# Gate products with adjacent moving columns, eleven row groups inside the first gates, and all modulation in mixer 1

## What is computed

```python
s = jnp.einsum('thpd,hpnd->thpn', q, sub_keys)          # two lists of 128 key scores a head
s_top, i_top = lax.top_k(s, PEER_TOPK)                  # 16 of each
best, pos = lax.top_k(cand, PEER_TOPK)                  # 16 pairs
expert = jnp.take_along_axis(cand_idx, pos, axis=-1)
g = jax.nn.softmax(best, axis=-1)
act = jax.nn.gelu(jnp.einsum('td,thkd->thk', xb, u[expert]), approximate=False)
return jnp.einsum('thk,thkd->td', g * act, v[expert])
```

## Time and profile before

| | |
|---|---|
| median of 3 runs | 3645.04 us (3644.92 to 3646.84) |
| profiled execution, its span | 3653.25 us, 3651.1 us |
| PE, DVE, POOL, ACT busy | 93%, 66%, 37%, 36% |
| DMA moved | 908.08 MB, mean 249 GB/s |
| mixer 1, heads 0 to 7 | about 252 to 490 us |
| queries and choice, first gates, block loop of layer 1 | 600 to 758, to 864, to 1870 us |
| first gates, block loop of layer 2 | 2525 to 2631, to 3642 us |

### The profile page before, as it was taken

The page is one execution under the profiler, slowest core; times in us unless marked ns, Lnnn a source line. Parts: engine busy times, 40 slices in busy tenths (PEclk is TensorE's granted clock), DMA queues, the critical chain, the costliest instruction groups (busy, mean ns, idle before and its releaser), DMA issues. The chain is left out here.

```text
span 3651.1 us, 44818 instructions
## 1 busy us (share of the span) xinstructions
PE 3378.0 (93%) x16120; PEld 2179.6 (60%) x16120; DVE 2419.8 (66%) x5203; ACT 1317.9 (36%) x3289; POOL 1343.6 (37%) x1028
## 2 busy tenths in 40 slices
PE   6986889989999999998979998996999999999988
PEld 3434644367777777765534465454867777777654
DVE  1038643876887987887771233269578798888778
ACT  2122111145655555541010134113555555555200
POOL 0000000003666667776620000000156566687665
PEclk9998689989999999999989998997799999999999
DMA  3211213225999999999961110211399999999998
GB/s 116 92 46 69 70 64 144 99 93 191 383 375 362 386 397 397 409 409 409 409 268 69 52 64 12 104 47 53 99 353 390 347 403 382 394 409 409 409 409 356
DMA packets 271692, 908.08 MB, mean 249 GB/s; under 512 B 30536, under 2 KB 31192, under 8 KB 270960
## 3 DMA queue, kind: packets, MB, share of 16 engines
q0 software_dynamic: 147456, 536.94, 37.7%
q1 hardware_dynamic: 124016, 368.29, 26.7%
HBM read 900.90 MB, written 4.22 MB: 248 GB/s over the span
## 5 line engine op out<-in xcount | busy, mean ns | idle before, releaser
L671 PE MATMUL psum<-hT,mod 128*128 128x256 f32 x4096 | 985.3, 396 | 55.3 <-ACT big L1088 29.5
L671 PEld LDWEIGHTS psum<-hT,mod 128*128 128x128 f32 x4096 | 796.4, 199 | 185.0 <-issue 77.9
L1098 ACT ACTIVATE levels<-key_numbers,hT 128x128 bf16<-128x128 f32 x1712 | 543.3, 389 | 452.5 <-PE psum L707 342.7
L1847 POOL DMA_INDIRECT w<-in_peer_u,tmp x172 | 243.1, 1414 | 978.8 <-DVEq L1543 791.1
L1676 DVE SCALAR_TENSOR_TENSOR tmp<-w,small,tmp 128x1024 f32<-128x1024 f32 x339 | 435.6, 1285 | 67.5 <-DMA w<-in_peer_v,tmp 27.6
L707 PEld LDWEIGHTS psum<-x,levels 128*128 128x128 bf16 x6144 | 384.2, 116 | 148.1 <-issue 120.2
L1656 DVE CUSTOM_DVE_ANT_0 w<-w,hn 128x1024 f32<-128x1024 f32 x342 | 407.6, 1224 | 57.8 <-DMA w<-in_peer_u,tmp 28.3
L707 PE MATMUL psum<-x,levels 128*128 128x32 bf16 x6144 | 405.8, 238 | 34.5 <-issue 14.1
L1847 POOL DMA_INDIRECT big<-in_peer_down,tmp x86 | 120.5, 1401 | 833.3 <-DVEq L1543 703.0
L681 PE MATMUL psum<-rows,big 128*128 128x512 f32 x800 | 358.8, 592 | 0.7 <-DVE big L1612 0.7
L1101 ACT ACTIVATE levels<-levels 128x512 bf16<-128x512 bf16 x428 | 269.6, 630 | 13.6
(11 more groups left out here) (303 smaller groups left out, 4082.3 us busy)
## 6 DMA issues: line engine op xcount, KB each, us to landing
mod<-in_uT SPq DMA_DIRECT2D x256, 512.0 KB
rows<-in_peer_v SPq DMA_DIRECT2D x64, 512.0 KB
rows<-in_peer_up SPq DMA_DIRECT2D x64, 512.0 KB
w<-in_w_in SPq DMA_DIRECT2D x14, 2048.0 KB, 7.9
w<-in_ada_w SPq DMA_DIRECT2D x12, 2048.0 KB, 8.0
srow<-in_peer_v SPq DMA_DIRECT2D x32, 512.0 KB
tmp<-in_peer_v SPq DMA_DIRECT2D x32, 512.0 KB
srow<-in_peer_up SPq DMA_DIRECT2D x32, 512.0 KB
```

What stands on the lines that cost most here:

```text
L671: last = nc.tensor.matmul(ps[4 + e % 2][:, 0:ND], ub[e % UV][:, k, :], hT[:, k, ND:SEQ], start=k == 0, stop=k == KC - 1)
L1098: last = nc.scalar.activation(hits[n % HITS][:, j * P:(j + 1) * P], keyno, ACT.Abs, bias=nibT[:, n * BATCH + j:n * BATCH + j + 1])
L1847: nc.gpsimd.indirect_dma_start(ring[n % ROWS], None, table, bass.IndirectOffsetOnAxis(idx[:, c:c + 1], 0))\
```

## The change

It does five things. (1) `hot` is laid out (part, token, key), so that the 32 moving columns of a token lie side by side. (2) For that, `first_keys` holds the first key's number and the gate along the innermost dimension, and the table `key_rows` with its one cast falls away. (3) Eleven of the 128 units run inside the first gates, one every fourth batch from batch 20 (`first_units`); `unit_table` spreads the other 117 over the loop, with its costs as they were. (4) All twelve sections of modulation stand in mixer 1: two behind each of heads 0 to 3, one behind heads 4 to 7. (5) Layer 1 then does as layer 2 did: eight first products instead of four before the gates.

```diff
+FIRST_UNITS = 11
-def blocks_before(layer, n):
-    first = 4 if layer == 0 else 8
-    return first + (AHEAD - first) * n // BATCHES
+def blocks_before(n):
+    return 8 + (AHEAD - 8) * n // BATCHES
+def first_units(n):
+    return max(0, min(FIRST_UNITS, (n - 16) // 4))
...
-    share = (4 * GROUPS * 5.15 + sum(v[1] for v in room)) / sum(v[0] for v in room)
+    share = ((4 * GROUPS - FIRST_UNITS) * 5.15 + sum(v[1] for v in room)) / sum(v[0] for v in room)
...
-    return [round(4 * GROUPS * v / done) for v in table]
+    return [FIRST_UNITS + round((4 * GROUPS - FIRST_UNITS) * v / done) for v in table]
+def after_head(h):
+    return (2 * h, 2 * h + 1) if h < 4 else (h + 4,)
...
-        hot = [part(x_, 8 + 3 * b, 3, BF16).rearrange("p (r a t) -> p r a t", r=3, a=QA) for b in range(2)]
+        hot = [part(x_, 8 + 3 * b, 3, BF16).rearrange("p (r t a) -> p r t a", r=3, a=QA) for b in range(2)]
...
-                                                hot[n // 4 % 2][:, r, :, t], start=r == 0, stop=r == 2)
+                                                hot[n // 4 % 2][:, r, t, :], start=r == 0, stop=r == 2)
...
# PE, mixer 1
-                modulation(h)
+                for n in after_head(h):
+                    modulation(n)
...
# PE, behind layer 1's queries
-            modulation(8)
-            modulation(9)
-            modulation(10)
-            turn_picks(0, 0)
-            modulation(11)
-            turn_picks(0, 1)
-            for e in range(4):
-                first_product(0, e)
+            first_experts(0)
...
# ACT, mixer 1
-                    if l == 6 and h:
-                        modulation(h - 1)
+                    if l == 5 and h:
+                        modulation(after_head(h - 1)[0])
...
                     if h >= 1:
                         head_out(h - 1, P, 0, h, wide_sq, h - 1)
+                        if h <= 4:
+                            modulation(after_head(h - 1)[1])
...
# DVE, first_keys
-                    spreads(tt(hot_one, key_rows, first_no[q][:, c].unsqueeze(1).to_broadcast([P, QA, WIDE]), ALU.is_equal))
-                    tt(hot[m % 2], hot_one.unsqueeze(1).to_broadcast([P, 3, QA, WIDE]),
-                       g_part[:, :, c].unsqueeze(2).to_broadcast([P, 3, QA, WIDE]), ALU.mult).then_inc(ga_ready, 1)
+                    spreads(tt(hot_one, keyno16[:, 0:QA].unsqueeze(1).to_broadcast([P, WIDE, QA]),
+                               spread(first_no[q][:, c], [P, WIDE, QA]), ALU.is_equal))
+                    tt(hot[m % 2], hot_one.unsqueeze(1).to_broadcast([P, 3, WIDE, QA]),
+                       spread(g_part[:, :, c], [P, 3, WIDE, QA]), ALU.mult).then_inc(ga_ready, 1)
...
# DVE, loop over the 64 batches of the first gates
                     for _ in range(first_pieces(n - 1), first_pieces(n)):
                         next(chooser[0])
+                    for u in range(first_units(n - 1), first_units(n)):
+                        run_unit(layer, u)
```

More of the change, by code:

```diff
@@ L403, in build @@
         ada = cols(a["ada_w_2"], 12)
-        ada_at = [len(order) + n + (6 if n >= NH else 0) for n in range(12)]
-        order += ada[:NH] + cols(a["w_out"], 2) + cols(a["peer_w_q"], 4) + ada[NH:]
+        ada_at = [len(order) + n for n in range(12)]
+        order += ada + cols(a["w_out"], 2) + cols(a["peer_w_q"], 4)
         order += cols(a["w_in_2"], 7) + cols(a["w_out_2"], 2) + cols(a["peer_w_query_2"], 4)
-        OUT_FIRST = (15, 32)
+        OUT_FIRST = (19, 32)
         outputs = [0 if n in ada_at else 4 for n in range(len(order))]
@@ L506, in _ @@
                 second_block(0, e)
-            for n in range(19, 23):
+            for n in range(23, 25):
                 load_section(n)
-            for n in range(NH, 12):
-                modulation(n)
             expert_blocks(0)
@@ L791, in modulation @@
                 seen.next(ada_row_in, 16)
-                nc.tensor.matmul(ps[1][0:1, :], ones[0:1, 0:1], ada_b[n // NH], start=False, stop=True).then_inc(ada_done, 1)
+                nc.tensor.matmul(ps[1][0:1, :], ones[0:1, 0:1], ada_b, start=False, stop=True).then_inc(ada_done, 1)
             full, heads = slice(0, P), [slice(0, 64), slice(64, P)]
@@ L899, in _ @@
             queries(1)
-            pe.wait_ge(sc_used, 32)
-            for e in range(6):
-                first_product(1, e)
-            turn_picks(1, 0)
-            turn_picks(1, 1)
-            first_product(1, 6)
-            first_product(1, 7)
+            first_experts(1)
             dense_experts(1)
@@ L1114, in group_gelu, with first_acts, unit_gelu @@
                 nc.scalar.activation(g8[g % 2], a8[g % 2], ACT.Gelu).then_inc(act_out, 1)
+            def first_acts(layer):
+                block_gelu(layer, 0)
+                block_gelu(layer, 1)
+                gate_exp(DENSE[0])
+                block_gelu(layer, 2)
+                gate_exp(DENSE[1])
+                block_gelu(layer, 3)
+                for n in range(len(DENSE)):
+                    copy_picks(layer, n)
+                for e in range(4, 8):
+                    block_gelu(layer, e)
+            def unit_gelu(layer, u):
+                kind, g = unit(u)
+                if kind == "u":
+                    group_gelu(layer, g)
             def dense_acts(layer):
@@ L1123, in dense_acts @@
                     if n >= 5:
-                        for e in range(blocks_before(layer, n - 5), blocks_before(layer, n - 4)):
+                        for e in range(blocks_before(n - 5), blocks_before(n - 4)):
                             block_gelu(layer, e)
@@ L1127, in dense_acts @@
                         gate_exp(0)
+                    for u in range(first_units(n - 6), first_units(n - 5)):
+                        unit_gelu(layer, u)
                 copy_gates(layer, 0, WIDES - 1)
-                for e in range(blocks_before(layer, BATCHES - 5), AHEAD):
+                for e in range(blocks_before(BATCHES - 5), AHEAD):
                     block_gelu(layer, e)
+                for u in range(first_units(BATCHES - 6), FIRST_UNITS):
+                    unit_gelu(layer, u)
                 for e in range(NKEY):
                     for u in range(units_due(e - 2), units_due(e - 1)):
-                        kind, g = unit(u)
-                        if kind == "u":
-                            group_gelu(layer, g)
+                        unit_gelu(layer, u)
                     if e and e + AHEAD - 1 < NKEY:
@@ L1153, in _ @@
             queries(0)
-            modulation(8)
-            modulation(9)
-            gate_exp(DENSE[0])
-            modulation(10)
-            gate_exp(DENSE[1])
-            copy_picks(0, 0)
-            modulation(11)
-            copy_picks(0, 1)
-            for e in range(4):
-                block_gelu(0, e)
+            first_acts(0)
             dense_acts(0)
@@ L1571, in peer @@
                 dve.wait_ge(x_stored, 32 * (layer + 1))
-                spreads(nc.vector.tensor_copy(key_rows, spread(keyno[:, 0:QA], [P, QA, WIDE])))
                 dve.wait_ge(picks_copied, len(DENSE) * (layer + 1))
@@ L1631, in peer @@
                     for n in range(units_due(e - 1), units_due(e)):
-                        kind, g = unit(n)
-                        if kind == "u":
-                            score_rows(layer, g)
-                        else:
-                            add_rows(layer, g)
-                            if g % GROUPS == GROUPS - 1:
-                                finish_tile(layer, g // GROUPS, y)
+                        run_unit(layer, n)
                 dve.wait_ge(blk_summed, (layer + 1) * NKEY)
@@ L1647, in peer, with run_unit @@
                         step(stt(x[:, t, :], x[:, t, :], rs[:, t:t + 1], rows[:, 2, :], ALU.mult, ALU.mult), 0 if t == NT - 1 else t)
+            def run_unit(layer, n):
+                kind, g = unit(n)
+                if kind == "u":
+                    score_rows(layer, g)
+                else:
+                    add_rows(layer, g)
+                    if g % GROUPS == GROUPS - 1:
+                        finish_tile(layer, g // GROUPS, y)
             def score_rows(layer, g):
```

52 lines of the change are left out of this document (24 added, 28 removed).

## The result

| | before | changed |
|---|---|---|
| median of 4 runs | 3644.98 us (3643.91 to 3646.84) | 3591.97 us (3590.15 to 3592.26) |
| ratio | | 0.9853, 95% interval 0.9836 to 0.987 |
| profiled execution, its span | 3653.25, 3651.1 us | 3592.14, 3590.3 us |

The change is faster by 53 us where 24 were predicted. Of the page of the changed kernel two lines, against the earlier trace rows: the GB/s, and the gathers' queue.

The account below looks back on a forecast made before the run. It took PE to bound each block loop up to step 92, DMA close behind, then DMA. Mixer -2, first gates +37 and +43, loops -51 each gave -24: 3621 us from the median, range 3592 to 3686.

Parts of the forecast that it names:

- Moving columns adjacent: Gate products in the loop: a pair of weight load and product falls from 60 to 40 ns, 0.48 us a batch.
- rival 1: Gate products stay at 60 ns a pair because the weight load sets it: +39, 3684 us, slower; chance 0.22.
- Gate held along the innermost dimension: On DVE, a first_keys goes from 1.45 to about 2.5 us, +1.07, 16 times in first gates, 48 in the loop.
- Eleven units in the first gates: First gates become DVE-bound and longer: +37 us in layer 1, +43 in layer 2.
- The loop without them: Block loop with the eleven units moved out: early stage gains 39 us, late stage 12, together -51 in each layer.
- Modulation: Mixer 1 with the moved sections: +10 us against PE's gains at heads 1 to 4, sum about -2.
- rival 3: The held gate costs DVE nothing for hot: 34 us less than forecast, 3587 us; chance 0.06.
- Rival 2: First gates pack badly, units delaying spreads PE needs: +38, so +14 in sum, 3659 us, slower; chance 0.12.
- Rival 4: Loop paced by POOL's fetches or single-row latency, not bytes; late stage gains nothing: 3645 us, no change; chance 0.1.

Follow-up runs that it names:

- the reads in eight ways: The changed kernel with PE reading its 32 moving columns in eight ways by turns in the later three quarters; 3608.7 us (one run).
- the pairs: The changed kernel with hot laid out (part, pair of tokens, key, token of the pair); 3552.4 us, 0.9731 of the kernel before.
- the cheap writer: The changed kernel, first_keys writing hot in the old layout with its fast forms, PE reading 32 adjacent elements; 3553.0 us, 0.9728 of the kernel before.
- the layout undone: The changed kernel with hot, key_rows, first_keys and the index in gates_of_batch as before the change; 3657.9 us, 1.0023 of the kernel before.

## Why the prediction was right in sign and too small in size

*Moving columns adjacent.* The reason was right, the size was not: this is the step that failed. "Between 27 and 60 I take 40, nearer the lower end but with something for the load" added a part for the load, for which the measured 25.4 ns leaves no room. The pair came even below the bound of 27, which was taken from fp32 columns. (The 13 ns for the load's columns set a shortest time, 97, against a median, 84; the shortest of the earlier trace rows is 79.) The Trainium skill (TensorE: Matmul & The Clock Gate, section "Back-to-back issue gap") states a floor of about 25 ns for up to 64 columns; the trace agrees with it at 25.4, and the prediction did not use it.

The rest of the step stands. It had PE as the bound up to step 49 and DMA behind it, and the trace shows PE full for the first 400 us and then 409 GB/s. Put 25.4 into it and the 104 batches of the first 49 steps take 104 x 12 x 14.6 ns = 18 us less, 718 for the 736; the measured shortening, 57 and 63 us of its 775, gives 718 and 711. The experiment makes it a little less: in the reads in eight ways 10.4 ns more a pair made each loop 9 us longer, so 14.6 ns are about 13 us. The early stage missed by 18 and 24 us. The remainder, 0 to 6 us a layer by the first working and 5 to 11 by the second, wasn't isolated; up to 8 us of it in all can be those by which the spans differ more than the medians. What also failed is the sentence under rival 1 that DMA takes over near 42 ns, by which a further fall would bring nothing: between 36 and 25 ns it still brought 9 us a loop.

*Gate held along the innermost dimension.* Right: 687 and 1758 ns for the predicted 689 and 1763. That it would cost the path in the first gates (17 us a layer in the sum, 14.6 by the pairs) and little in the loop is shown by the cheap writer and the pairs.

*Eleven units in the first gates.* Right in size: +40.7 us for +43 in layer 2; in layer 1 +35.1 for +37, the 36.8 of the table less the 1.7 of mixer 1. DVE was at 107 of 114.8 us, and the clock nearer its lower level. What the step didn't do was to set this price against the gain of the same eleven units alone: once the products are at 25 ns it comes out at a loss of 12 us, and in the sum it was hidden behind the layout's gain.

*The loop without them.* The late stage came at -10.9 and -9.1 for -12. The early one is the term above.

*Modulation.* -2 was forecast, +1.7 measured at the end of mixer 1. The forecast's own terms give 10 - 4.5 - 6, about -0.5 and not -2. Heads 1 to 4 begin 5.4, 5.7, 7.6 and 7.9 us later than before, where the terms give 5.5 by head 4: the 1.5 us taken for each of heads 1 to 3 didn't come. Head 4 gained 3.7 us (29.0 to 25.3) for the 6 taken. Over the whole kernel the place of the modulation makes no measurable difference.

*The rivals.* Rival 1 (the load sets the spacing) falls with 25.4 ns. Its sum for 60 ns was good, though: +39, less the 34 of rival 3 for the held gate, is +5, and the layout undone came at +8. Rival 2 (first gates pack badly) falls too: the last 114.8 us of the stage hold 107 of DVE's work. Rival 3 falls, and is almost what the pairs then made true: it had 3587 from the predicted 3621, 34 us less, and the pairs measured 39. Rival 4 falls: the loop's late stage shrank and the loops follow the bytes at 3.9 to 4.1 us a unit of 2.1 MB, not the 5.1 of their bytes. PE's own work comes close behind, 112 x 3.53 + 128 x 3.43 + 192 x 0.305 = 893 us of the 929; that this keeps back the rest is likely and not shown.

## What to carry to other kernels

Read a matmul's moving columns so that few 16-byte lines of SBUF are touched, and look for a layout in which every operand of the DVE operation that writes them still has an innermost step of 1: here a run of two bf16 elements serves both. Count the lines with the offset, since a short run that crosses a line costs two. Price each part of a change by itself at the new bound and not at the old one; here one part carried the whole gain and another took some of it back. Work that is moved into a stage to fill an idle resource costs what it takes of that stage's full one, so compare the price of a unit in both places before moving it.

## What was not expected of the hardware

- A pair of weight load and product with 32 bf16 columns follows the last one by 25.4 ns, although the load alone is shown with 96 ns and the product with 176.
- The shown duration of a weight load fell with the moving columns' layout, its own operand unchanged: 97/117/118 ns to 95/96/98. These durations hold something of what stands beside them and are no price.
- The loop, though DMA is at 409 GB/s for half of it, gives back only 4 us for a unit whose bytes take 5.1.
- Two columns to a 16-byte line are not enough to hide the price of a new line (33 ns for 25.4), and a run of 2 that crosses into the next line costs the pair 60 ns for 30.
